# A 1-core kernel of two transformer blocks: residual tiles of the second block split before they are normalised

## The reference, cut to what matters

```python
h = rms_norm_2(x, mix_norm_g[layer])
z = h @ w_in                                   # layer 0: hgrn2 mixer, layer 1: MLA mixer
...
x = x + jnp.concatenate([y, m], axis=-1) @ w_out[layer]
x = x + conv_ffn(rms_norm_2(x, ffn_norm_g[layer]), w_up[layer], conv_w[layer], conv_b[layer], w_down[layer])

def rms_norm_2(x, g):
    xf = x.astype(jnp.float32)
    y = xf * lax.rsqrt(jnp.mean(xf * xf, axis=-1, keepdims=True) + EPS)
    return (y * g.astype(jnp.float32)).astype(x.dtype)

def conv_ffn(h, w_up, conv_w, conv_b, w_down):
    u = h @ w_up
    u = depthwise_conv(u, conv_w) + conv_b     # 3 taps along the tokens
    a, b = u[..., :D_FF], u[..., D_FF:]        # D_FF = 2816
    return (jax.nn.silu(a) * b) @ w_down
```

## Time and profile before

| | us |
|---|---|
| median of 3 runs (1914.97 to 1920.12) | 1918.17 |
| the profiled execution | 1913.36 |
| its span, first to last instruction | 1911.6 |
| PE busy | 1761.6 (92%) |
| PE weight loads busy | 1427.1 (75%) |
| DVE busy | 896.7 (47%) |
| ACT busy | 738.3 (39%) |
| POOL busy | 703.8 (37%) |

### The profile page before, as it was taken

The page is one execution under the profiler, slowest core; times in us unless marked ns, Lnnn a source line. Parts: engine busy times, 40 slices in busy tenths (PEclk is TensorE's granted clock), DMA queues, the critical chain, the costliest instruction groups (busy, mean ns, idle before and its releaser), DMA issues.

```text
span 1911.6 us, 24595 instructions
## 1 busy us (share of the span) xinstructions
PE 1761.6 (92%) x8605; PEld 1427.1 (75%) x8605; DVE 896.7 (47%) x1623; ACT 738.3 (39%) x1122; POOL 703.8 (37%) x362
## 2 busy tenths in 40 slices
PE   6999899996799898798999999989977989999999
PEld 4778566885678787676888888868855768888887
DVE  4587565457522255755444432253355554444200
ACT  4332465223453344414445432134424244544322
POOL 2334111443325565032444444532200324444444
PEclk9999999998899898888999999988988989999999
DMA  4232211242223110012323333322100222333333
GB/s 175 88 110 89 66 34 45 89 132 77 89 67 103 60 48 23 12 56 66 99 88 99 99 99 110 99 72 70 63 12 1 67 66 88 99 99 99 99 100 120
DMA packets 43275, 151.71 MB, mean 79 GB/s; under 512 B 4928, under 2 KB 5056, under 8 KB 43072
## 3 DMA queue, kind: packets, MB, share of 16 engines
q1 hardware_dynamic: 41184, 145.16, 23.8%
q10 hardware_dynamic: 2016, 5.53, 0.8%
HBM read 148.58 MB, written 2.10 MB: 79 GB/s over the span
## 4 chain that ended last, share of the span: by engine, by line
issue 52%; PE 24%; POOL 20%; DVE 1%; ACT 1%; DMA 1%; POOLq 0%; ACTq 0%; DVEq 0%
POOL WL L528 20%; PE DB L607 4%; PE DB L609 4%; PE DB L608 4%; PE SC L893 2%; PE SC L707 1%; PE DB L732 1%; PE DB L657 1%; PE DB L659 1%; PE DB L658 1%; PE OB L721 1%; PE TB L607 1%; PE DB L721 1%; PE OB L919 1%; DMA CONST<-in_consts_dram 1%
## 5 line engine op out<-in xcount | busy, mean ns | idle before, releaser
L528 POOL TENSOR_TENSOR WL<-RAW,WH 128x1024 fp32r<-128x1024 f32 x268 | 647.6, 2417 | 1187.1 <-ACT WH L1090 1187.1
L1090 ACT ACTIVATE WH<-RAW 128x1024 fp32r<-128x1024 f32 x268 | 284.0, 1060 | 794.3 <-PE DB L609 300.3
L960 PE MATMUL DB<-XH,WH 128*128 128x512 f32 x704 | 277.4, 394 | 6.3 <-DVE XL L1499 6.3
L961 PE MATMUL DB<-XL,WH 128*128 128x512 f32 x704 | 275.8, 392 | 0.0
L962 PE MATMUL DB<-XH,WL 128*128 128x512 f32 x704 | 275.6, 391 | 0.0
L607 PE MATMUL DB<-XH,WH 128*128 128x512 f32 (+1 forms) x552 | 231.6, 419 | 14.0 <-DVE XL L1499 9.0
L608 PE MATMUL DB<-XL,WH 128*128 128x512 f32 (+1 forms) x552 | 218.8, 396 | 0.0
L609 PE MATMUL DB<-XH,WL 128*128 128x512 f32 (+1 forms) x552 | 218.1, 395 | 0.0
L960 PEld LDWEIGHTS DB<-XH,WH 128*128 128x128 f32 x704 | 132.9, 189 | 39.3 <-DVE XL L1499 7.5
L962 PEld LDWEIGHTS DB<-XH,WL 128*128 128x128 f32 x704 | 133.3, 189 | 27.9
L961 PEld LDWEIGHTS DB<-XL,WH 128*128 128x128 f32 x704 | 133.3, 189 | 27.1
(11 more groups left out here) (384 smaller groups left out, 3018.4 us busy)
## 6 DMA issues: line engine op xcount, KB each, us to landing
RAW<-in_stream_dram SPq DMA_DIRECT2D x268, 512.0 KB, 3.5
TP<-in_toep_dram ACTq DMA_DIRECT2D x4, 512.0 KB, 3.7
out_dram<-X SPq DMA_DIRECT2D x8, 256.0 KB, 4.3
X<-in_xt_dram ACTq DMA_DIRECT2D x4, 256.0 KB, 5.2
X<-in_xt_dram SPq DMA_DIRECT2D x4, 256.0 KB, 4.7
MRAW<-in_memt_dram ACTq DMA_DIRECT2D x1, 1024.0 KB, 6.9
CONST<-in_consts_dram ACTq DMA_DIRECT2D x1, 448.0 KB, 9.7
MSKI<-in_masks_dram ACTq DMA_DIRECT2D x1, 288.0 KB, 3.6
```

Source lines behind the costliest of these rows:

```text
L528: nc.gpsimd.tensor_tensor(WL[:, s, :], RAW[:, j, :], WH[:, s, :].bitcast(F32), ALU.subtract).then_inc(lo_done, 1)
L960: mm(o, WH[:, s, c], xh(k), start=(k == 0), stop=False)
L961: mm(o, WH[:, s, c], xl(k), start=False, stop=False)
L1090: A(WH[:, n % SPLIT, :], RAW[:, n % RING, :], ACT.Copy).then_inc(hi_done, 1)
```

## The change

In the second block a residual tile is split as soon as its bank is finished, without the factor, and the factor multiplies what the next jobs give:
- `late_tile` on ACT and `late_low` on DVE. DVE adds `X` to the finished bank in place. ACT reads the bank three times: `XH = bank * gain`, the square into `SQ`, and a copy back to `X`. DVE makes `XL = bank * gain - XH` from the bank, which empties it, and adds the square to a sum that lies in the PSUM bank `SC[1]`.
- PE starts the first job behind the seam with a wait for each tile's `XL` (`dve_emptied`), then does `norm_sum`. The spread comes after 4 of the 8 tiles of the second job. `ua_0`, `ub_0`, `ua_1`, `ub_1` stand in front of the loop, which starts at turn 1. The drain of PE behind the `wo` jobs is gone; the one behind the `dn` jobs stays.
- DVE copies the spread factor out of `SC[1]`, to `SQ[:, 0]` (FFN) or to the new `ROOT1` (seam 5). In the FFN loop it multiplies each job's bank by it, in place, and ACT's first tap waits for that (`scaled`) and no longer for `slab_used`.
- Behind seam 5 DVE and not ACT empties the banks of `cq`, `ckv`, `kpe`, `qm1`, multiplying by `ROOT1` (`scaled_out`): the three `cq` ahead of the angles, the two `ckv` behind them, `kpe` behind the split of `cq`, `qm1` behind the split of `ckv`. ACT only runs the slabs' `high` there, and waits for `dve_emptied` before it squares.
- The square of a tile is now made by ACT, in the seams too, and the squares' sum on DVE no longer has two inputs in SBUF.

The diff, cut to its core:

```diff
@@ -132,12 +132,12 @@
     ffn(0)
     assert at_ % 4 == 0
     for k in range(3):
-        add(f"cq{k}", 1, 1, KD, "act")
+        add(f"cq{k}", 1, 1, KD, "dve")
...
@@ -159,7 +159,8 @@
 SQB = {0: 0, 1: KD, 3: 2 * KD}
 ACC = {0: 0, 1: KD - 1, 2: 2 * (KD - 1), 3: 2 * KD - 1, 4: 3 * KD - 2, 5: 3 * KD - 1, 6: 3 * KD}
-XLB = {0: 0, 1: KD, 3: 3 * KD, 4: 4 * KD, 5: 5 * KD, 6: 6 * KD}
+XLB = {0: 0, 1: KD, 3: 3 * KD}
+LATE = {4: 0, 5: KD, 6: 2 * KD}
 def plan_heads():
...
@@ -301,6 +302,7 @@
         POSI = at("POSI", [P, TOK], A0 + 84, I32)
         KPR = at("KPR", [P, TOK], A0 + 60)
+        ROOT1 = at("ROOT1", [P, TOK], A0 + 28)
         HALF = [slice(0, DH), slice(DH, P)]
         def keys_and_queries(h, m):
...
@@ -939,15 +948,19 @@
                 for k in range(KD):
                     feature_job(f"wo{l}{k}", hi, lo, inputs=inputs if k == 0 else None)
-                pe.drain().then_inc(arena_free, 1)
+                feature_job(f"ua{l}_0", xh, xl, inputs=lambda j: emptied(f"wo{l}{j}", dve_emptied))
                 norm_sum(ni)
-                norm_spread(ni)
+                for k, _ in enumerate(feature_tiles(f"ub{l}_0", xh, xl)):
+                    if k == 3:
+                        norm_spread(ni)
+                feature_job(f"ua{l}_1", xh, xl)
+                feature_job(f"ub{l}_1", xh, xl)
                 ja = JOBS[f"ua{l}_0"]
                 s0, u0 = ja.slabs[0], ja.banks[0]
-                d0 = EMPTIED[BEFORE[u0]][1]
-                with pe.Fori(0, FF // 2) as it:
+                d0 = EMPTIED[u0 - 4][1]
+                with pe.Fori(1, FF // 2) as it:
                     for j in range(4):
                         pe.wait_ge(dve_emptied, it * 4 + (d0 + j))
                         pe.wait_ge(lo_done, it * 4 + (s0 + j + 1))
@@ -955,8 +968,6 @@
                         for k in range(KD):
                             c = slice(P * k, P * k + P)
                             o = DB[j][:, :]
-                            if j == 0:
-                                pe.wait_ge(xl_done, XLB[ni] + k + 1)
                             mm(o, WH[:, s, c], xh(k), start=(k == 0), stop=False)
                             mm(o, WH[:, s, c], xl(k), start=False, stop=False)
                             last = mm(o, WL[:, s, c], xh(k), start=False, stop=(k == KD - 1))
@@ -987,10 +998,12 @@
             tail(0, lambda j: YH[:, j, :], lambda j: YL[:, j, :], 4,
                  lambda j: (hs_done, HEADS["ho5"][0] + 1) if j < HG else (o_out, j + 3))
+            feature_job("cq0", xh, xl, inputs=lambda j: emptied(f"dn0{j}", dve_emptied))
             norm_sum(5)
-            norm_spread(5)
-            for k in range(3):
-                feature_job(f"cq{k}", xh, xl, xready=XLB[5] if k == 0 else None)
+            for k, _ in enumerate(feature_tiles("cq1", xh, xl)):
+                if k == 3:
+                    norm_spread(5)
+            feature_job("cq2", xh, xl)
             for k in range(2):
                 feature_job(f"ckv{k}", xh, xl)
             feature_job("kpe", xh, xl)
...
@@ -1128,6 +1141,13 @@
                         act.wait_ge(xt_done, base + k + 1)
                         A(XH[:, k, n * l:n * l + n], TMP[:, k % 2, 0:n], ACT.Copy).then_inc(xh_done, 1)
+            def late_tile(k, dk, b, gain):
+
+                act.wait_ge(sum_made, k + 1)
+                A(flat(XH[:, dk, :]), DB[b][:, :], ACT.Identity, scale=gain)
+                A(SQ[:, b % 2, :], DB[b][:, :], ACT.Square)
+                A(flat(X[:, dk, :]), DB[b][:, :], ACT.Copy).then_inc(x_back, 1)
+
             def norm_rest(ni):
                 norm_std(ni)
                 norm_high(ni)
...
@@ -1360,8 +1380,10 @@
             attention(segments["m0"])
             def tail(l, ni):
-                split_past(f"wo{l}{KD - 1}")
-                norm_rest(ni)
+                for k in range(KD):
+                    split_past(f"wo{l}{k}")
...
@@ -1372,7 +1394,7 @@
                             j = 2 * jj + e
                             w = CW[:, l, bass.ds(it * 2 + jj, 1), :].rearrange("p o c -> p (o c)")
                             high(s0 + j + SPLIT, it, 4)
-                            act.wait_ge(slab_used, it * 4 + (s0 + j + 1))
+                            act.wait_ge(scaled, it * 4 + (2 * base + j + 1))
                             A(dst[:, jj, :], DB[j][:, :], ACT.Identity, scale=w[:, 4 * e + 2:4 * e + 3],
...
@@ -1383,28 +1405,32 @@
                 with act.Fori(0, KD // 4) as it:
                     for j in range(12):
                         high(s0 + j + SPLIT, it, 12)
+                        if l == 0 and j % 3 == 2:
+                            k, g = it * 4 + (LATE[5] + j // 3), COLS["mix1"][0] + j // 3
+                            late_tile(k, bass.ds(it * 4 + j // 3, 1), j // 3, PAR[:, bass.ds(it * 4 + g, 1)])
                 split_next[0] = s0 + 3 * KD + SPLIT
             tail(0, 4)
-            act.wait_ge(arena_free, 4)
+            act.wait_ge(arena_free, 3)
             act.dma_start(POSI[:, :], pos_in.partition_broadcast(P)).then_inc(pos_ready, 16)
-            norm_rest(5)
-            for k in range(3):
-                evac(f"cq{k}", CQ[:, k, :])
-            for k in range(2):
-                evac(f"ckv{k}", CKV[:, k, :])
-            act.wait_ge(act_emptied, EMPTIED[JOBS["ckv1"].banks[0]][1])
+            split_past("cq0")
+            norm_std(5)
+
+            def left(name):
+                split_past(name)
+                act.wait_ge(dve_emptied, EMPTIED[JOBS[name].banks[0]][1])
+
+            left("ckv1")
             for k in range(3):
                 head_square(HEADS["cq"][1][k], CQ[:, k, :])
             group_std("cq", 1.0 / 384, 0)
-            evac("kpe", KPE[:, :])
+            split_past("kpe")
             for k in range(2):
                 head_square(HEADS["ckv"][1][k], CKV[:, k, :])
-            evac("qm10", QM1[:, 0, :])
+            split_past("qm10")
             group_std("ckv", 1.0 / 256, 0)
...
@@ -1530,6 +1556,15 @@
                 if k:
                     last = V.tensor_tensor(PB[:, 2, :], PB[:, 2, :], sq, ALU.add)
                     link(last) if k < KD - 1 else last.then_inc(acc_done, 1)
+
+            def late_low(k, dk, b, gain):
+
+                dve.wait_ge(x_back, k + 1)
+                V.scalar_tensor_tensor(flat(XL[:, dk, :]), DB[b], gain, flat(XH[:, dk, :]).bitcast(F32), ALU.mult, ALU.subtract
+                                       ).then_inc(dve_emptied, 1)
+                if not isinstance(k, int) or k:
+                    dve.wait_ge(squared, k)
+                V.tensor_tensor(SC[1][:, :], SC[1][:, :], SQ[:, b % 2, :], ALU.add).then_inc(squared, 1)
...
@@ -1822,12 +1857,19 @@
             attention(segments["m0"], head_outputs())
             def tail(l, ni, gain):
+                link(V.memset(SC[1][:, :], 0.0))
                 for k in range(KD):
-                    add_to_x(f"wo{l}{k}", k)
-                dve.wait_ge(arena_free, {0: 3, 1: 6}[l])
-                x_norm(ni, gain)
+                    j = JOBS[f"wo{l}{k}"]
+                    dve.wait_ge(slab_used, j.done)
+                    V.tensor_tensor(DB[j.bank()], DB[j.bank()], X[:, k, :], ALU.add).then_inc(sum_made, 1)
+                    late_low(LATE[ni] + k, k, j.bank(), col(gain, k))
+                dve.wait_ge(squared, LATE[ni] + KD)
+                V.tensor_copy(PB[:, 2, :], SC[1][:, :]).then_inc(acc_done, 1)
+                dve.wait_ge(std_done, ni + 1)
+                norm_root(ni)
+                link(V.tensor_copy(SQ[:, 0, :], SC[1][:, :]))
                 ja = JOBS[f"ua{l}_0"]
-                u0, base, c0 = ja.banks[0], FF * l, chain[0]
+                s0, u0, base, c0 = ja.slabs[0], ja.banks[0], FF * l, chain[0]
                 d0 = EMPTIED[u0][1]
                 V.drain().then_inc(cv_g, 2)
@@ -1836,6 +1878,8 @@
                         pair = it * 2 + (base + jj)
                         for e, dst in ((0, SB), (1, PB)):
                             j = 2 * jj + e
+                            dve.wait_ge(slab_used, it * 4 + (s0 + j + 1))
+                            V.tensor_tensor(DB[j], DB[j], SQ[:, 0, :], ALU.mult).then_inc(scaled, 1)
                             y, u = dst[:, jj, :], DB[j]
                             w = CW[:, l, bass.ds(it * 2 + jj, 1), :].rearrange("p o c -> p (o c)")
...
@@ -1856,27 +1900,33 @@
                         V.tensor_tensor(gl, TMP[:, jj, :], gh.bitcast(F32), ALU.subtract).then_inc(g_done, 1)
                 chain[0] = c0 + 6 * (FF // 2)
                 jd = JOBS[f"dn{l}0"]
-                s0, u0, c1 = jd.slabs[0], jd.banks[0], chain[0] + 1
-                link(V.memset(PB[:, 2, :], 0.0))
+                s0, u0 = jd.slabs[0], jd.banks[0]
+                if l == 0:
+                    link(V.memset(SC[1][:, :], 0.0))
                 with dve.Fori(0, KD // 4) as it:
                     for j in range(4):
                         dve.wait_ge(slab_used, it * 12 + (s0 + 3 * j + 3))
```

(36 more changed lines are left out.)

21 lines of the change are left out of this document (14 added, 7 removed).

## The result

The changed kernel takes 1887.97 us (median of 4 runs, 1882.08 to 1888.45) against 1919.08 (4 runs, 1914.97 to 1920.12): a ratio of 0.9846, 95% interval 0.9819 to 0.9872, 31.1 us faster. Its profiled execution took 1888.45 with a span of 1886.6, 25.0 us less than the one shown of before.

A forecast was written before the change was run, and what follows sets the result against it. PE bounds the kernel, busy 1761.6 of 1911.6 us. Gains 22.8 (seams 4 and 6) + 14.4 (seam 5) - 3.8 - 5.0 (clock) = 28.4; profiled 1885.0, plus 4.8 to the median: 1889.8, range 1880 to 1901.

The forecast's parts named there:

- Seams 4 and 6: From the last old matmul to ua_1: length falls from 27.33 to 15.9 us, a gain of 11.4 in each.
- The new wait: At ua_1 in seams 4 and 6, PE waits 3.1 us for weights queued on ACT behind the spread factor's copy.
- its rival: A table load holds ACT longer than its own 1.28 us, both ua_1 waits grow by 1.3: 1892.4; chance 0.02.
- what would show it: Profile signs listed beforehand, among them a 3.1 us wait for POOL L528 at ua_1 and no gaps in the FFN loops.
- Late tiles: First job behind the seam: the eighth tile comes 0.7 us early, and the sum of squares costs no wait.
- Behind seam 5: Bank emptying moved to DVE behind other work gives back 3.8 us, as 3.3 + 0.5.
- (a): Behind seam 5, the two ckv wait for DVE's angles: just in time, 0.5 us taken for collisions with POOL.
- (b): Behind seam 5, kpe goes ahead of ckv's reciprocal on DVE: 0.7 us later.
- (c): Behind seam 5, both qm1 go behind the split of ckv: their sum of squares 3.3 us late, (b) included.
- "slower" rival: FFN half turn becomes a chain of 6.9 + 2D us against 10.87; at 2.71, 64 us lost, 1954; chance 0.03.
- D: Time of DVE's multiplication in PSUM in the FFN loops, taken as 0.69 us, 2.71 if it collides with POOL.
- The clock: PE's clock falls behind the new wait in each of seams 4 and 6: 2.5 us each, 5.0 in all.

The follow-up runs named there:

- e1_high_first: Against the changed kernel, ScalarE splits the weights of ua_1 before it makes the standard deviation, not inside the loop: 1878.31 us, ratio 0.9803 to the kernel before.
- e6_one_extra: Against the changed kernel, one extra multiplication stands ahead of each multiplication by the norm factor in the FFN loops: 1888.57 us, ratio 0.9846 to the kernel before.
- e7_late_last_tile: Against the changed kernel, ScalarE makes two more squares between the last wo tile's addition and its XH in seams 4 and 6: 1878.35 us, one execution.

## Why the prediction was right, and where not

*Seams 4 and 6.* Right, within 0.4 us each: 16.33 against 15.9. The new wait was forecast at 3.1 and is 3.20, by the chain that the prediction gave (copy, drain, load, `high`, POOL). The load is followed 1.30 us after its start by the next activation (878.63, 879.93), so the price by the earlier trace rows held. The drain of some 1380 ns that the Trainium skill, "ScalarE: Activation LUTs", section "What ACT_TABLE_LOAD costs", adds to a load, and which would have made each seam 1.4 longer, didn't come: its rival falls. Nor does one stand ahead of a load: in the loop of the changed kernel an activation of 0.76 us starts at 930.03, a load at 930.81 and the next activation at 932.11. What I had short is 0.3 in all: half a job behind the partition sum took 2.87 (873.70 to 876.57) instead of 2.72, as the first of its matmuls start up to 0.33 apart instead of 0.23, and from the first matmul of the spread to the copy out of the bank on DVE 1.09 went by (876.57 to 877.66) instead of 0.88. The profile puts the wait down to DVE and not to POOL, against "what would show it".

*Late tiles.* No wait, as said; the room was 1.2 instead of 0.7 for the tile, 0.5 for the sum of squares.

*DVE with its output in PSUM.* 0.69 was taken between bounds of 0.69 and 2.71:

```profile
L1882 DVE TENSOR_TENSOR DB<-DB,SQ 128x512 f32<-128x512 f32 x88 | 61.3, 697 | 50.6 <-PE DB L973 42.7 <-PE DB L618 7.1 <-DVE SQ L1870 0.7
```

*Seam 5.* The gain was 13.5, not 14.4. Three small terms: the first matmul comes 0.65 behind the last instead of 0.50, the matmuls beside the small ones are slower, and the spread waits 0.24 for `RS`, since DVE's copy took 0.93 here and 0.43 in seam 4.

*Behind seam 5.* 3.8 was forecast, and the three waits come to 3.74: (a) 1.33, (b) 0.47 (a spread's wait went from 1.04 to 1.51) and (c) 1.94, in each of the five profiles with this order (two of the changed kernel, `e1_high_first`, `e6_one_extra`, `e7_late_last_tile`). In the first profile of the changed kernel, with the spread of before behind them:

```profile
1270.53 2.84 PE L685 MATMUL SC<-CONST,SQ 128*128 128x1 f32 x24 [1.33 <-ACT SQ L1163]
1290.26 1.16 PE L692 MATMUL OB<-CONST,SB 128*128 128x128 f32 x8 [1.51 <-DVE SB L1589]
1297.47 1.95 PE L685 MATMUL SC<-CONST,SQ 128*128 128x2 f32 x16 [1.94 <-ACT SQ L1163]
```

```profile
1312.13 1.16 PE L683 MATMUL OB<-CONST,SB 128*128 128x128 f32 x8 [1.04 <-DVE SB L1554]
```

The total was right and its split was not, so part of it is luck. (a) was put at 0.5: the angles, from 1253.52 on, take 15.1 us and not 13.1, with three operations of one SBUF input at 2.50 that take 0.43 elsewhere. One of them:

```profile
1254.50 2.50 DVE L1937 TENSOR_SCALAR PB<-PT 128x512 f32<-128x512 f32 x1
```

I had priced only two-input operations as able to collide with POOL. (b) and (c) are 2.4 us of waiting, in the place forecast (`qm1`'s squares behind `uqn0`), against 3.3. The window grew by 2.7 in the first pair of profiles and by 3.5 in the mean, with 5.9 and more between single executions. The clock falls several times in this window in both kernels, with and without the new waits, and not in the same places: in four of the five profiles PE runs at 1.2 GHz right behind (c) and so comes later to a wait of 1.35 that every profile of before has there, and that wait is gone.

*FFN loops.* No gap in them, as said, and the clock is at 1.00. But the bound behind the "slower" rival was wrong: 6.9 was 7.77, and the overlap of `GL` with POOL adds 1.7 to 1.9 once the chain is late. It decides at D = 1.55 instead of 2.0, and at 2.71 it would have cost about 170 us instead of 64, an estimate between the 115 at 2.13 and the 183 at 2.85. I had priced DVE's chain with ACT's busy times and left out that a longer chain moves ACT's `high` and so POOL's work onto DVE's.

*The clock.* One fall behind each of the two new waits, as said; each costs 1.7 us, the lower end of what I had from the earlier trace rows (1.7 to 3.4), not 2.5. The clock in the seams rose from 0.75 to 1.00.

*The sum.* 28.4 us was forecast for the profiled pair and 25.0 came: the seams gained 1.7 less than said, the clock cost 1.6 less, the work behind seam 5 1.1 less (in this pair), and 3.9 and 0.4 were lost where no term was, in the attention and the front. The attention's part is chance: the profile of before happened to have the short one. *From span to median* I added 4.8 us, the distance between before's profiled execution and its median. For the changed kernel this distance is -0.5. So 3.4 too much gain met 5.3 too much offset. On medians the gain is 31.1 and on the profiles 25.0; the executions of before are spread over more than this difference: its four profiled ones took 1904.2 to 1914.4 us, its others 1912.9 to 1920.1, with clocks of 0.949 to 0.954 where they are on record. Why the profiled ones lie low stays open. So that the forecast came within 2 us is luck in part; what the runs bear out is the gain in the seams. The range's lower end had a slip as well: the reasons given for 1880 come to 1883.2.

*"What would show it".* One sign was wrongly stated: "no wait of PE for L1531". The row has its longest wait, 14.8 us, in an earlier stage that the change doesn't touch, and it is still there:

```profile
PE SC L685 <- DVE PB L1557: 14.8, 1, 14.8
```

The seams' part of that row was 23.4 - 14.8 = 8.6 us. The sum didn't use the row, only the windows, and so wasn't hurt.

## What to carry to other kernels

A factor that multiplies a whole row can be moved behind the next product: the matmuls then start on raw tiles, and the seam shrinks to the small matmuls. Look then for what was ordered by the old wait: a weight preparation that stands in an engine's queue behind the factor (here 2.83 us and a clock fall of 1.7 at each of two seams), and banks that are emptied behind unrelated work (here 3.7 us of new waits, and 4.8 us of waits gone with another order). Price a loop's spare time by its chain, from one start to the next with the wait taken out, and not by busy shares; and ask which two operations a delay pushes onto each other.
